# GpSimd issues the 192 transfers that arrange the neighbourhood bias in the second attention of the first block, not in the first

## The reference

```python
def first_block(x, ...):
    for i in range(DEPTH):           # kinds 0, 1, 2, 0
        if kind == 0: y = short_conv_mixer(...)
        elif kind == 1: y = dsa_mixer(...)
        else: y = mla_mixer(...)
        x = x + y
    return x

def neighborhood_attention(q, k, v, k_ctx, v_ctx, rpb):
    ...
        bias = rpb[:, dr_idx][:, :, dc_idx]
        s_loc = jnp.einsum('bqhd,bkhd->bhqk', q_r, k_b) * scale + bias
        s_loc = jnp.where(band_mask, s_loc, NEG_INF)
    ...
```

## Time and profile before

| | |
|---|---|
| time, median of 3 runs | 3208.28 us (3207.35 to 3209.14) |
| the profiled execution's own time | 3210.21 us |
| its span in the trace | 3208.4 us |
| PE busy | 3088.7 us, 96% |
| DVE busy | 1676.8 us, 52% |
| POOL busy | 1502.0 us, 47% |
| ACT busy | 944.3 us, 29% |
| mean granted TensorE clock | 0.984 |

### The profile page before, as it was taken

How to read it: one execution, slowest core, us unless ns; L and a number is a source line. 1 busy time by engine, 2 the same in 40 slices (tenths; PEclk the granted TensorE clock), 3 DMA queues, 4 the chain that set the end, 5 groups by cost and what they waited for, 6 DMA issues and landing times.

```text
span 3208.4 us, 40231 instructions
## 1 busy us (share of the span) xinstructions
PE 3088.7 (96%) x15372; PEld 2027.0 (63%) x15516; DVE 1676.8 (52%) x3462; ACT 944.3 (29%) x1464; POOL 1502.0 (47%) x788
## 2 busy tenths in 40 slices
PE   8999998898999999997998999999999999999998
PEld 6888785687677877885776444666655444444444
DVE  6433698548754341007424998444441255556664
ACT  2001225424641011115122223333333322222222
POOL 4664469755035664565556333333333333333331
PEclk9998999999999999998999999999999999999999
DMA  3222122123323222221223344444444656655551
GB/s 142 105 83 105 55 103 54 40 82 114 128 103 114 96 99 105 92 105 47 79 105 132 131 157 157 168 187 196 193 179 190 226 206 209 209 207 200 196 195 65
DMA packets 139832, 429.99 MB, mean 134 GB/s; under 512 B 8640, under 2 KB 79424, under 8 KB 116544
## 3 DMA queue, kind: packets, MB, share of 16 engines
q1 hardware_dynamic: 125216, 353.40, 30.9%
q10 hardware_dynamic: 7200, 68.68, 5.1%
q0 software_dynamic: 7296, 6.31, 0.8%
HBM read 358.10 MB, written 73.40 MB: 134 GB/s over the span
## 4 chain that ended last, share of the span: by engine, by line
PE 83%; DVE 11%; ACT 3%; issue 2%; DMA 1%; POOL 0%; SPq 0%; ACTq 0%; DVEq 0%; POOLq 0%
PE bank L1084 14%; PE bank L1085 14%; PE bank L1086 14%; PE bank L1107 4%; PE bank L653 4%; PE bank L648 4%; PE bank L649 4%; PE bank L676 3%; PE bank L681 3%; PE bank L677 3%; PE bank L907 3%; PE bank L902 3%; PE bank L903 3%; ACT work L1383 1%; DVE hF L1728 1%
## 5 line engine op out<-in xcount | busy, mean ns | idle before, releaser
L2398 POOL TENSOR_TENSOR work<-ring,work 128x4096 bf16<-128x4096 f32 x64 | 531.1, 8298 | 905.0 <-ACT work L1529 905.0
L1085 PE MATMUL bank<-work 128*128 128x512 bf16 x2004 | 761.2, 380 | 11.3 <-POOL work L2398 9.1
L1084 PE MATMUL bank<-work 128*128 128x512 bf16 x2005 | 761.7, 380 | 5.8 <-DVE work L2236 2.8
L1086 PE MATMUL bank<-work 128*128 128x512 bf16 x1991 | 756.1, 380 | 2.3
L2422 POOL CAST w_parts<-ring 128x1024 fp32r<-128x1024 f32 (+3 forms) x212 | 233.2, 1100 | 657.5 <-DMA ring<-in_wstream 156.7
L2424 POOL TENSOR_TENSOR w_parts<-ring,w_parts 128x1024 fp32r<-128x1024 f32 (+3 forms) x212 | 515.7, 2433 | 17.0
L2236 DVE TENSOR_TENSOR work<-hF,work 128x512 bf16<-128x512 f32 x128 | 307.7, 2404 | 253.0 <-ACT work L1613 249.9
L1084 PEld LDWEIGHTS bank<-work 128*128 128x128 bf16 x2048 | 200.8, 98 | 246.9 <-issue 14.0
L1086 PEld LDWEIGHTS bank<-work 128*128 128x128 bf16 x2048 | 200.8, 98 | 242.9 <-issue 2.2
L1085 PEld LDWEIGHTS bank<-work 128*128 128x128 bf16 x2048 | 200.7, 98 | 235.5 <-issue 1.7
L1529 ACT ACTIVATE work<-ring 128x4096 bf16<-128x4096 f32 x64 | 231.5, 3617 | 207.4 <-PE bank L1086 179.8
(11 more groups left out here) (341 smaller groups left out, 4967.9 us busy)
## 6 DMA issues: line engine op xcount, KB each, us to landing
ring<-in_wstream SPq DMA_DIRECT2D x128, 2048.0 KB, 7.7
hidden<-hF ACTq DMA_DIRECT2D x32, 1024.0 KB, 3.9
gates<-work ACTq DMA_DIRECT2D x16, 2048.0 KB, 8.3
hF<-hidden SPq DMA_DIRECT2D x32, 1024.0 KB, 6.7
work<-gates SPq DMA_DIRECT2D x32, 1024.0 KB, 10.1
rpb_tiles<-in_rpb POOLq DMA_DIRECT2D x192, 16.0 KB, 2.5
work<-rpb_tiles POOLq DMA_DIRECT2D x24, 128.0 KB, 4.1
ring<-in_wstream SPq DMA_DIRECT2D x5, 512.0 KB, 3.9
```

The lines of the kernel that those rows point to most:

```text
L1084: pe.matmul(out, a(0), b(0), start=(start and k == 0), stop=False)
L1085: pe.matmul(out, a(0), b(1), start=False, stop=False)
L1086: mm = pe.matmul(out, a(1), b(0), start=False, stop=(stop and k == n - 1))
L2398: nc.gpsimd.tensor_tensor(SPLIT[:, p, 1, :], ring[:, p, :], SPLIT[:, p, 0, :], ALU.subtract).then_inc(lo, 1)
```

## The change

One call is moved in GpSimd's list, from ahead of `b_out` to ahead of `c_out`. Nothing is added or removed; the 192 transfers, their semaphore and their reader stay the same. The chunks of `b_out` now follow those of `b_in` directly.

```diff
@@ -2432,7 +2432,6 @@
             weight_parts("b_idx", 1, KT, 72, 4, 1, 4)
             weight_parts("b_in", 2, KT, 512)
             weight_parts("b_in", 6, KT, 512, 2, 2, 8)
-            arrange_bias()
             weight_parts("b_out", 2, KT, 512)
             weight_parts("c_lat", 1, KT, 416, 2)
             weight_parts("c_lat", 1, KT, 256, 4, 1, 4)
@@ -2441,6 +2440,7 @@
             weight_parts("c_uq", 4, 3, 384, 2)
             weight_parts("c_z", 1, KT, 512, 0, 1, 0, "c_z1")
             weight_parts("c_uv", 2, 2, 512, 2)
+            arrange_bias()
             weight_parts("c_out", 2, KT, 512)
             weight_parts("a_in1", 8, KT, 512)
             first_biases()
```

## The result

| | kernel before | changed kernel |
|---|---|---|
| median, 20 executions each | 3207.51 us (3205.11 to 3222.03) | 3214.79 us (3208.60 to 3233.42) |
| ratio | | 1.0032, 95% interval 1.0018 to 1.0045 |
| the profiled execution's own time | 3210.21 us | 3208.60 us |
| its span in the trace | 3208.4 us | 3206.8 us |
| mean granted TensorE clock | 0.984 | 0.985 |

A forecast was written before the change was run, and what follows sets the result against it. PE carries 83% of the chain, but DVE sets attention b's barrier and pace, so GpSimd work matters through collisions. Terms -3.7 + 6.1 + 0 + 0 = +2.4 us on 3208.28 gave 3210.7 us, range 3205.0 to 3214.5.

The forecast's parts named there:

- Term 2: Ahead of attention b's barrier: two b_out chunks on GpSimd collide with DVE, the last comer; +6.1 us.
- +4.5 us by a full 8.2 us: Upper bound ahead of the barrier: DVE blocked for the whole 8.2 us of GpSimd's four operations, less 3.7.
- Term 1: End of attention b: the b_out chunks no longer collide with DVE's score tiles in the last units; -3.7 us.
- Term 3: Attention c: the 192 transfers delay c_out's first chunk some 0.6 us, still covered by PE-paced units; 0 us.
- Term 4: What issuing the transfers costs other engines, ring loads and the reader `first_biases`; 0 us, bounds ±0.5.
- The slow issuing: Rival, attention c: DVE keeps GpSimd from writing transfers, which go one by one; about +71 us, some 3282; chance 0.04.
- the short cover in attention c: Rival: issuing ends late, c_out's chunks run into units paced by DVE; +3.7 us more, 3214.4; chance 0.08.
- within 0.2%: Whole kernel: measured time the same as before, within about 0.2% or 6.4 us; chance 0.89.

The follow-up runs named there:

- same_as_before: The kernel before, unchanged, handed in as if it were a changed one; 3208.0 us, ratio 0.9992.
- bfill_before: Kernel before plus 6 PE products that compute nothing, in the pause ahead of attention b's barrier; 3207.90 us, ratio 1.0001.
- fill_before: Kernel before plus idle PE products: 6 ahead of attention b's barrier, 3 in the wait ahead of the c_z1 products; 3205.17 us, ratio 0.9979.
- late_c: Kernel before with the 192 transfers moved to attention c, b_out's first two chunks held at their old place; 3211.73 us, ratio 0.9997.
- cfill_before: Kernel before plus 3 idle PE products in the wait for GpSimd ahead of the c_z1 products; 3208.43 us, ratio 0.9999.
- again: The changed kernel run once more, unchanged; 3213.33 us, ratio 1.0008 to the kernel before.
- early_b: Kernel before with b_out's first two chunks straight behind b_in, the 192 transfers staying in attention b behind them; 3214.09 us, ratio 1.0014.
- nudge_after: Changed kernel plus one PE product that computes nothing (0.87 us) at the start of b_out; 3214.99 us, ratio 1.0022 to the kernel before.
- cfill_after: Changed kernel plus 3 idle PE products ahead of the c_z1 products; 3212.69 us, ratio 1.0009 to the kernel before.
- fill_after: Changed kernel plus idle PE products, 13 ahead of attention b's barrier and 3 ahead of c_z1; 3211.15 us, ratio 1.0001 to the kernel before.
- barrier_c: Kernel before with the 192 transfers moved to attention c and b_out's first two chunks behind attention b's barrier; 3211.44 us, ratio 0.9998.
- barrier_b: Kernel before with b_out's first two chunks behind attention b's barrier, the 192 transfers behind them in attention b; 3208.69 us, ratio 0.9995.
- c fillers: 3 idle PE products in the wait ahead of c_z1; they take 2.2 +- 1.2 us from the changed kernel, 0.3 +- 0.7 from the one before.
- fill_barrier: Kernel before with b_out's first two chunks behind attention b's barrier, transfers behind them, 6 and 3 idle PE products in two waits; 3204.46 us, ratio 0.9974.

## Why the prediction was wrong

Forecast 3210.7 us with a range up to 3214.5; measured 3214.79, just above it. The collisions were where the prediction had them; what it made of their sum, and of the spread of the kernel, was not.

- **Term 2, the chunks ahead of the barrier: +6.1 predicted, +5.8 measured**, in six traces alike. The casts start at 489.32 and 494.75, where 489.6 and 495.1 were given; PE waits 11.89 us where 12 was given. The clock comes back 11 to 12 us into the attention in both (0.57 in 511 to 513 us and 1.00 behind it before, 0.59 in 516 to 518 us and 1.00 behind it now), so the work at the lower level stayed the same, as said. The first chunk met other operations than its row, and cost the same. The rule of the Trainium skill quoted in the prediction ("SBUF — State Buffer", "Who interferes with whom") agrees with the trace: the first L1847 ends only behind the cast (0.91 us), a later one only behind the subtraction (2.38 us). Its sum, +4.5 us by a full 8.2 us, did not come about. In the trace DVE had an operation of its own under way when each cast began (L1838 from 489.18, the cast from 489.32; L1835 from 494.57, the cast from 494.75), and L1836 ended between the second chunk's cast and the end of its subtraction.
- **Term 1, attention b: -3.7 predicted, -3.9 in the pair of traces.** The last unit is 12.06 us. But the kernel before was given by one trace. Its five other traces with the chunks at the end of attention b and no delay (same_as_before, bfill_before, fill_before, late_c, cfill_before) take 0.9, 0.4, 1.7 and 1.1 us less there, and the last 0.1 more. With the trace of before counted in that is -0.7 us on average, and the six traces with the change's order (changed kernel, again, early_b, nudge_after without its filler of 0.87 us, cfill_after, fill_after) average -3.7: what the change gives back is 3.0 us.
- **Term 3, the cover in attention c: 0 predicted, 0 measured.** Units of 16.09 us, `c_out` at 927.15 - 610.89 = 316.26 us behind `b_out` where it was 925.50 - 609.37 = 316.13 us. The pause in issuing was 3.03 us and did not come twice.
- **Term 4, the transfers' other costs: 0 predicted;** changed kernel less early_b -0.4 +- 1.0 us, barrier_c less barrier_b +1.0 +- 1.0, late_c less before +2.3 +- 0.8: nothing or a little, not settled. The slow issuing that the Trainium skill warns of ("SBUF — State Buffer", "SBUF: two separate sides") did not occur: 0.527 us a transfer beside attention c, where 0.68 was the point from which it would have counted.

**The step that failed is the sum.** It put -3.7 from one execution against +6.1 and stopped at +2.4 us. Term 1 was too large: over six traces of each order it is 3.0 us and not 3.7, so these two stretches make 5.8 - 3.0 = +2.8 us, and the means say +3.9 +- 0.6. The sum also took the clock at nothing ("from nothing to 1 us. I take nothing"), and let it only help. In fact three stretches of this kernel vary from execution to execution: attention b by 1 to 2 us and, with the clock, "sum c" by 4.5 us and what lies behind `c_out` by 5 us. Counted from L1836 to the end of the span, the six traces with the change's order take 3.4 +- 1.1 us more than the six with the old one (+5.8, -3.0, 0.0 in "sum c" and +0.7 behind `c_out`). That agrees with the means, and what they have beyond +2.8 us isn't clear of the noise. If the changed kernel had the costly case of c in two executions of three and the one before in one of three, that would be 4.5 / 3 = 1.5 us more. The c fillers point that way, but the traces don't: two of the six of each order have it (again and early_b; bfill_before and late_c). So the last microsecond is argued and not shown. That barrier_b and barrier_c, some 4 us better in their two stretches, are no better in time is the same question from the other side; it too is open.

**Where the 4.1 us between 3210.7 and 3214.79 come from.** The three first runs of the kernel before lay 0.6 us under its mean (3208.28 and 3208.9). The change cost 3.9 us in place of 2.4, which is 1.5. And the median of the 20 executions lies 1.9 us above the mean of 12 of them (3212.86), because the other 8 are of the upper group. Of all executions of the changed kernel 10 of 32 are, and the difference of the means with every execution counted is 6.6 +- 1.4 us. In the kernels with the change's order it is 25 of 91 together, in all others 49 of 320. Whether the change makes this group more frequent, or 8 of 20 was chance, is open: in the traces the clock's fall lies ahead of what the change touches, and no run tests it.

**The range failed with it.** Its upper end was the price of one rival mechanism, the short cover in attention c, which did not come about. The spread that each kernel has between executions was not in it: the changed kernel's profiled execution, for one, lay 4 us under the mean. The chances fared as little: "within 0.2%" had 0.89, and the first measurement gave 0.32% (0.18 to 0.45), the second 0.08% (-0.10 to 0.27).

## What to carry to other kernels

A GpSimd operation on 128x1024 that has begun holds up a DVE product with both inputs in SBUF until it ends, however small DVE's own operation is: four of them, 7.9 us together, cost DVE 5.8 us here. So work on GpSimd that has slack belongs where DVE isn't what the next barrier waits for; a set of DMA issues, beside which DVE's operations took no longer here, is a good thing to have there instead. A difference of a few microseconds in 3200 is not to be read from one trace of each kernel: count the same stretch in several traces of both, and let its spread, and that of the stretches the change doesn't touch, into the range. Filling a pause of TensorE with products that compute nothing is worth a try when they fit: 0.26% here together with the chunks behind the barrier.

## What the runs showed of the hardware that was not expected

- Four products of 128x32 on DVE, 0.50 us together, took 3.42 us beside one cast and one subtraction on GpSimd. What a collision cost here was set by the longer partner.
- A float32 product of 128x128 by 128x512 takes 0.87 us and counts as two matrix instructions (36 for 18); the estimate of 0.59 us a piece, from the row of a single-pass product, let the fillers overrun their pause.
- After the same wait of 3.07 us, the same products ran at 0.39 us each in one execution and at 0.63 us in another, by the granted clock (1.00 and 0.67 in the window of 760 to 768 us). In the five traces in which PE was given work in that wait, the costly case did not occur; without it, it did in six of 15.
- Keeping TensorE busy ahead of the barrier of attention b gained 2.1 +- 1.0 us in the mean of the kernel before (bfill_before; its ratio, 1.0001, shows none), though the barrier came at the same time. In the windows above, the clock behind attention b is 1.00 in fill_barrier and 0.89 in the trace of before; that the gain comes from there wasn't tested by itself.
